# Writing the low parts of split weights with two half-width subtractions instead of one

## What is computed

```
def token_mixer(h, h0, on_grid, p):
    u = h @ p['w_in']                                   # 1024 x 7168
    b_c, c_c, v_c, x_r, g_r, m_a, m_b = jnp.split(u, IN_SPLITS, axis=-1)
    y_a = (b_c * conv_over_tokens(c_c * v_c, ...)) @ p['w_conv_out']
    x_c = conv_over_tokens(x_r, p['rnn_conv_w'], ...) + p['rnn_conv_b']
    h_f, last_f = rg_lru(x_c, ..., False)               # gates, exp, sqrt, scan forward
    h_b, last_b = rg_lru(x_c, ..., True)                # the same backward
    y_b = ((h_f + h_b) * gelu(g_r)) @ p['w_rnn_out']
    merged = sigmoid(m_a) * y_a + sigmoid(m_b) * y_b
    return merged @ p['w_o'], ...

def hier_moe(h, p):                                     # 32 experts, top 1 group, top 2 experts
    for e in range(N_EXPERTS):
        z = silu(t @ p['w1'][e]) * (t @ p['w3'][e])
        y = y + gates[:, e:e + 1] * (z @ p['w2'][e])
```

## Time and profile before

| What | Value |
|---|---|
| Time, median of 3 runs (lowest, highest) | 961.01 us (960.68, 962.0) |
| Time of the profiled execution | 960.13 us |
| Its span in the profile | 958.2 us |
| TensorE busy, share of the span | 887.8 us, 93% |
| VectorE busy | 595.8 us, 62% |
| ScalarE busy | 283.3 us, 30% |
| GpSimd busy | 291.9 us, 30% |
| Mean granted TensorE clock | 0.992 of full speed |

### The profile page before, as it was taken

The page is one execution under the profiler, slowest core; times in us unless marked ns, Lnnn a source line. Parts: engine busy times, 40 slices in busy tenths (PEclk is TensorE's granted clock), DMA queues, the critical chain, the costliest instruction groups (busy, mean ns, idle before and its releaser), DMA issues.

```text
span 958.2 us, 12628 instructions
## 1 busy us (share of the span) xinstructions
PE 887.8 (93%) x4502; PEld 551.3 (58%) x4502; DVE 595.8 (62%) x987; ACT 283.3 (30%) x499; POOL 291.9 (30%) x232
## 2 busy tenths in 40 slices
PE   3998999999999999999999999998999899989895
PEld 1688988888899999855443444343333333433331
DVE  2589977596602642235477777676666666757677
ACT  4475373736234432112311212111111111212112
POOL 0046626253455555222311221321313121213100
PEclk9999999999999999999999999999999999999999
DMA  9962545563665248445799999999999999999991
GB/s 344 355 249 90 181 170 182 176 215 137 208 231 176 94 150 301 170 188 219 289 400 409 410 417 411 417 424 401 412 391 414 399 403 390 405 394 409 403 416 78
DMA packets 61867, 285.70 MB, mean 298 GB/s; under 512 B 6880, under 2 KB 11264, under 8 KB 47477
## 3 DMA queue, kind: packets, MB, share of 16 engines
q1 hardware_dynamic: 58212, 278.63, 75.2%
q0 software_dynamic: 2480, 3.11, 1.1%
q10 hardware_dynamic: 1120, 3.24, 0.9%
HBM read 286.80 MB, written 3.19 MB: 303 GB/s over the span
## 4 chain that ended last, share of the span: by engine, by line
PE 58%; DMA 23%; DVE 10%; ACT 3%; issue 2%; SPq 1%; POOL 0%; DVEq 0%; ACTq 0%
DMA ring<-in_w 13%; DMA slot<-in_w 10%; PE bank L1106 10%; PE bank L884 8%; PE bank L886 8%; PE bank L885 8%; PE bank L1123 7%; PE bank L952 4%; PE bank L1107 3%; PE bank L1083 2%; PE bank L820 2%; DVE xcy L1709 1%; PE bank L1061 1%; SPq L633 1%; PE bank L830 1%
## 5 line engine op out<-in xcount | busy, mean ns | idle before, releaser
L475 POOL TENSOR_TENSOR subs<-ring,subs 128x1024 fp32r<-128x1024 f32 x69 | 175.6, 2552 | 214.1 <-ACT subs L1255 214.1
L884 PE MATMUL bank<-h_hl,subs 128*128 128x384 f32 x488 | 166.5, 341 | 7.1 <-POOL subs L475 4.1
L885 PE MATMUL bank<-h_hl,subs 128*128 128x384 f32 x488 | 164.2, 337 | 0.0
L886 PE MATMUL bank<-h_hl,subs 128*128 128x384 f32 x488 | 164.2, 336 | 0.0
L2050 DVE TENSOR_TENSOR lru<-bank,cp 128x512 f32<-128x512 f32 x186 | 116.2, 677 | 57.6 <-PE bank L1083 57.5
L1106 PE MATMUL bank<-ring,x_T 128*64 128x512 f32 x256 | 120.1, 611 | 12.5 <-DMA slot<-in_w 4.9
L1107 PE MATMUL bank<-ring,x_T 128*64 128x512 f32 x256 | 118.7, 605 | 0.0
L2059 DVE TENSOR_TENSOR hg<-hg,lru 128x512 f32<-128x512 f32 x186 | 116.6, 679 | 0.0
L671 POOL COPY idx<-lists 64x1 uint32 (+1 forms) x31 | 5.5, 177 | 309.1 <-PE bank L1061 304.5
L884 PEld LDWEIGHTS bank<-h_hl,subs 128*128 128x128 f32 x488 | 91.7, 188 | 13.6 <-issue 9.6
L1106 PE MATMUL bank<-slot,x_T 128*64 128x512 f32 x192 | 89.3, 606 | 9.2 <-DMA slot<-in_w 6.7
(11 more groups left out here) (248 smaller groups left out, 1467.7 us busy)
## 6 DMA issues: line engine op xcount, KB each, us to landing
ring<-in_w SPq DMA_DIRECT2D x40, 2048.0 KB, 28.7
slot<-in_w SPq DMA_DIRECT2D x30, 2048.0 KB, 28.8
ring<-in_w_in SPq DMA_DIRECT2D x14, 2048.0 KB, 8.2
ring<-in_w_ada SPq DMA_DIRECT2D x12, 2048.0 KB, 9.0
gate_w<-in_w SPq DMA_DIRECT2D x10, 2048.0 KB, 29.9
ring<-in_w SPq DMA_DIRECT2D x16, 1024.0 KB, 30.9
slot<-in_w SPq DMA_DIRECT2D x12, 1024.0 KB, 31.3
ring<-in_w_rnn_out SPq DMA_DIRECT2D x2, 2048.0 KB, 8.4
```

The lines of the kernel that those rows point to most:

```text
L475: eng.tensor_tensor(pair[:, 1], src, pair[:, 0].bitcast(F32), ALU.subtract).then_inc(done, 1)
L884: eng.matmul(ps[:, 0:T], pair[:, 1, k, :], x[:, 0, k, :], start=(k == 0), stop=False)
L885: eng.matmul(ps[:, 0:T], pair[:, 0, k, :], x[:, 1, k, :], start=False, stop=False)
L886: mm = eng.matmul(ps[:, 0:T], pair[:, 0, k, :], x[:, 0, k, :], start=False, stop=(k == KD - 1))
```

## The change

`write_lo` writes the low part of a quarter with two subtractions instead of one: the first takes blocks 0 to 3 of the 8 (512 elements of each partition), the second blocks 4 to 7. Only the second signals. Nothing stands between the two. It holds for VectorE's three quarters and GpSimd's 69.

```
             src, pair = quarter(q)
             eng.wait_ge(hi_ready, q + 1)
-            eng.tensor_tensor(pair[:, 1], src, pair[:, 0].bitcast(F32), ALU.subtract).then_inc(done, 1)
+            for ks in (slice(0, KD // 2), slice(KD // 2, KD)):
+                last = eng.tensor_tensor(pair[:, 1, ks], src[:, ks], pair[:, 0, ks].bitcast(F32), ALU.subtract)
+            last.then_inc(done, 1)
```

## The result

The changed kernel takes 954.8 us (median of six runs, 953.6 to 955.82) where the kernel before, run beside it, takes 961.37 (960.25 to 965.48). The ratio is 0.9925, 95% interval 0.9906 to 0.9945: faster by about 7 us. The forecast was 958.8 in a range of 954.5 to 964.0. The sign and the range held; the forecast change of 2.2 us was about a third of the measured one (6.6 us by these medians, 7.2 by the ratio).

A forecast was written before the change was run, and what follows sets the result against it. Up to 250 us, GpSimd's subtractions hold up VectorE, for which TensorE waits. L1748's -3.3 us and +1.1 us for the price of a half made -2.2, from a median of 961.01 to 958.8 us; range 954.5 to 964.0.

The forecast's parts named there:

- The mechanism: GpSimd and VectorE take turns between the two halves, so VectorE waits for one half only; faster overall, 0.5 chance.
- the rival of the halves that are not parted: GpSimd runs both halves without letting VectorE in: +5.2 us, 966.2 us; nearly all of the 0.2 chance for slower.
- L1748's term: In gate batches 1 to 3, L1748 waits for one half instead of a whole subtraction: 3 x 1.11 = -3.3 us.
- The price of a half: From 50 to 250 us, 38 quarters meeting VectorE cost +0.03 us each, +1.1 us, with ends -3.8 and +6.1.
- The ceiling: TensorE's waits in the projections: at most 10.6 us to win, of which its waits for VectorE cap at 6.5.
- more than that: At -0.10 us a quarter the sum is -7.1 us, capped at 6.5 by TensorE's waits for VectorE: 954.5 us.
- The rival in which the hand-over eats the gain: Extra turn changes at 0.09 us each, or low parts late at 77 us, leave 960.5 to 961.1 us; chance 0.3.
- The lateness: Low parts finish up to 1.67 us later, covered or taken up by TensorE's other waits: 0, other end +1.7 us.
- VectorE's three: VectorE's own three low-part subtractions, ending at 47.93 us, fall in idle time even when split: 0.
- SyncE's queue: Ring slots come free and loads are issued up to 1.67 us later, covered by the four-chunk ring: 0.
- the quarters from 250 us on: Quarters after 250 us meet a full TensorE and a GpSimd with 52.9 us to spare: 0.
- Stalls from 50 to 127 us: VectorE's stall sums there stay within 2 us of before; growth above 3.4 us would refute the forecast's half price.

## Why the sign was right and the size was not

**The mechanism held.** The engines take turns between two subtractions with nothing to wait for between them: L1750 at 2.74 us (forecast 2.8), scans at 1.97 to 2.01 (forecast 2). So the rival of the halves that are not parted is out. The Trainium skill, "GPSIMD Engine Reference", section "2.1 Instruction dispatch", has the engine's cores go on to the next instruction as soon as their own share is done; the trace shows that this does not keep VectorE out, since L1750 got its turn after one half.

**L1748's term held**: -3.3 forecast, -2.8 (-4.3 to -1.3) by the kernel that splits these three quarters alone, with the reservation on batch 1 made there.

**The price of a half was the step that failed.** The prediction wrote "Where VectorE always has a next instruction, splitting saves nothing by itself" and took +0.03 us for each of 38 quarters, +1.1 us. Measured, the term has the other sign: with the other quarters alone the runs show gains of 2.5 us (0.9 to 4.0) in the second stretch and of 3.0 (1.2 to 4.8) in the first, and the changed kernel's 7.2 us less L1748's 2.8 leave 4.4. Three things stand in the place of that price. A quarter beside the scans costs about 0.1 us less in halves than whole, the lower bound of -0.10 that the forecast had and set aside. Where VectorE's next instruction reads a bank, it goes on beside a half, and less than a turn is left to wait for; in batch 2 three quarters cost 4.25 us in place of 6.35. And the count of 38 was itself not fixed: ScalarE releases a quarter every 4 us or so, and a VectorE that is a few us ahead has finished its part before the next one comes, 2 us for each quarter slipped past, in each of batches 1 to 3. That third term follows from the other gains and multiplies them: in batch 3 neither L1748's half nor the other halves brought it alone. The shares are read from the three batches; the first stretch was not taken apart in this way, and why its gain is above what was expected stays open.

**The ceiling decided the size.** With that, VectorE gained 3.5 us in batch 1, 1.1 + 4.4 in batch 2 and 3.5 in batch 3, more than the 1.43, 1.99 and 1.42 us that TensorE waited there, and what goes beyond the wait is worth nothing. All 6.5 us of waits for VectorE went. With those for GpSimd (4.1 to 3.9) and the new 0.3 for ScalarE the waits fell by 6.4 us, the span of the profiled executions by 6.5. That these two agree so well is partly luck: a wait costs more than its length in the list, and against that stand the 0.5 us of the later start and 1.5 us of a low clock behind the wait at 80 us (last section). So 6.5 us is no hard cap, as the prediction took it to be, and neither are the 10.6 us that it starts from; the ratio's interval goes from 5.3 to 9.0 us. This is the case that the prediction called "more than that" and priced at 954.5 by the same cap. It reached it by -0.10 us a quarter alone; the traces show that this was the smallest of the three contributions in batch 2. That the range holds the measured time, 0.3 us inside its low end, is therefore in part luck. The rival in which the hand-over eats the gain, within 1.9 us of before, is out by the interval of the ratio.

**The lateness was judged rightly where it would have decided.** TensorE has no wait at 139, 185 or 231 us. Its waits at 77 and 87 us were to grow in sum and be taken up: the one near 80 us grew by 0.9 us, but that at 87 us is gone, so the sum fell from 2.7 to 2.03; the one near 55 us, which the forecast left out, grew by 0.5. In batch 1 the low part's row ends at 133.61 + 4.70 = 138.31; the forecast's 138.64, moved by the 0.33 us by which the batch starts earlier, is the same. The kernel with quarters 3 and 7 whole has the same time within some 2 us, so no cost of this lateness shows; its wait came back at 89 us.

**VectorE's three, SyncE's queue and the quarters from 250 us on** were set at nothing. The first was measured at 0.12% (0.01% to 0.23%) less time, under the 0.2% below which the prediction calls a change none; for the others, no wait of TensorE appeared between 80 and 402 us.

**Stalls from 50 to 127 us** were to stay within 2 us: VectorE's busy time there fell from 74.25 to 72.39, within that bound, and the 1.75 us of TensorE's waits at 122 and 125 went with it.

## What to carry to other kernels

Where two engines shut each other out for the length of an instruction, as here, cut the instructions of the engine that is not on the path, so that the other waits for a part only; count as well what a small lead lets it slip past, since the next long instruction has its own release time. The worth is bounded by the waits at the end of the chain, each with the restart behind it, so read these first. Finer parts helped no more here once those waits were gone, and they moved time from the engine that is served to the one that is cut, until that one was late.

## What the runs showed of the hardware

A wait of TensorE cost more than its length in the list. In the kernel before, the last product ahead of the wait of 1.43 us starts at 154.17, the next ones at 155.94 and 156.22, where products otherwise start 0.17 us apart: 156.22 - 154.17 - 2 x 0.17 = 1.7 us lost.

A low clock can come on top, and in these runs it came in some executions and not in others. Behind the 2.03 us wait at 80 us the granted clock of the next 5 us was 0.66 in two profiles of the changed kernel and 1.00 in a third. The row of the table by stretch of the first:

```profile
80.00:85.00 5.00, 5.00 (x21) 5.00 (x21) 4.86 (x6) 1.31 (x4) 2.54 (x2) 0.66 0.85 303
```

There, matmuls of 0.34 us took 0.52 us, with TensorE at the lower of its two levels (1.2 GHz), and ten times the next one came 0.32 us after the last in place of 0.17: 1.5 us. In the kernel with three quarters in halves it was 0.66 from 125 to 130 us, behind a wait of 1.39 us that left it at 1.00 in the kernel before: four gate products took 2.89 us in place of 1.57. It came without a wait too, behind 32 products of 36 columns that took 3.66 to 3.75 us, with 0.83 from 340 to 350 us in three of the kernels and 1.00 in others, where the same products took 3.66 us. That the waits cause it is therefore not shown. So one profile of such a kernel can be a microsecond or two off another of the same kernel, and the timed runs have to decide.
